# Two model blocks in one kernel on one core: plain first output tiles in RG-LRU, another order of NSA's value exchange, fourth rotation and first attention steps, and early output products

## What is computed

```python
def rglru_mixer(h, w_in, conv_w, conv_b, w_ra, b_ra, w_ix, b_ix, lam, w_out):
    u = h @ w_in                          # 1024 x 3072
    xb, yb = u[..., :D_RNN], u[..., D_RNN:]      # D_RNN = 1536
    y = jax.nn.gelu(yb)
    ...                                   # conv, two gates, a and b_t from them
    def step(hprev, inp):
        a_t, b_t = inp
        hn = a_t * hprev + b_t
        return hn, hn
    _, hs = lax.scan(step, ...)
    return (rec * y) @ w_out              # rec is hs; 1536 x 1024

def nsa_mixer(h, w_q, gate_bias, w_o, kc, vc, ks, vs, kw_pad, vw_pad):
    # 16 heads, 4 key groups; q rotated in its first 24 of 96 dims for two branches
    ...                                   # per head and block of 128 queries:
    return g_t[..., 0:1] * o_c + g_t[..., 1:2] * o_s + g_t[..., 2:3] * o_w
    ...
    return o @ w_o                        # 1024 x 1024

def moba_mixer(h, w_qkv, q_gain, k_gain, w_out):
    ...                                   # 8 heads of 128, softmax over all keys at this length
    return o @ w_out
```

## Time and profile before

| | us |
|---|---|
| runs | 1742.52, 1743.94, 1744.46 |
| the profiled execution, whole | 1750.02 |
| its span, first to last instruction | 1748.2 |
| PE busy | 1709.4 (98%), 12958 instructions |
| PEld busy | 1603.4 (92%) |
| DVE busy | 1273.3 (73%) |
| ACT busy | 838.3 (48%) |
| POOL busy | 377.2 (22%) |
| mean granted clock of PE | 0.990 |
| DMA | 321 MB, 184 GB/s in the mean |

### The profile page before, as it was taken

The page is one execution under the profiler, slowest core; times in us unless marked ns, Lnnn a source line. Parts: engine busy times, 40 slices in busy tenths (PEclk is TensorE's granted clock), DMA queues, the critical chain, the costliest instruction groups (busy, mean ns, idle before and its releaser), DMA issues.

```text
span 1748.2 us, 31974 instructions
## 1 busy us (share of the span) xinstructions
PE 1709.4 (98%) x12958; PEld 1603.4 (92%) x12958; DVE 1273.3 (73%) x1667; ACT 838.3 (48%) x1110; POOL 377.2 (22%) x425
## 2 busy tenths in 40 slices
PE   7989999999999999999999999999999999999999
PEld 7779999898779999899989989998999989989998
DVE  7898889785858988888766867666666665676663
ACT  5865444443555444454444245444444444554442
POOL 0223012535405123510032121002100127330000
PEclk9999999999899999999999999999999999999999
DMA  8236568675205778555646334554455545335561
GB/s 322 97 117 214 197 216 274 226 271 194 69 1 178 257 243 292 190 182 180 228 157 242 136 139 175 192 206 178 158 181 203 205 153 176 117 130 193 193 226 37
DMA packets 50712, 321.03 MB, mean 184 GB/s; under 512 B 7696, under 2 KB 8912, under 8 KB 20144
## 3 DMA queue, kind: packets, MB, share of 16 engines
q1 hardware_dynamic: 36432, 280.61, 45.4%
q0 software_dynamic: 12736, 36.87, 6.5%
q10 hardware_dynamic: 1440, 2.10, 0.3%
HBM read 307.39 MB, written 10.09 MB: 182 GB/s over the span
## 4 chain that ended last, share of the span: by engine, by line
PE 89%; DVE 7%; ACT 2%; issue 1%; DMA 1%; POOL 0%; ACTq 0%; DVEq 0%
PE bank L2276 18%; PE bank L2270 17%; PE bank L2271 17%; PE bank L2272 17%; PE bank L2277 9%; DVE w_lo L1445 2%; PE bank L2529 1%; PE bank L2712 1%; PE bank L2880 1%; PE bank L2832 1%; PE bank L2601 1%; PE bank L2539 1%; PE bank L2450 1%; DMA vc_other<-vc_raw 1%; ACT w_hi L1019 1%
## 5 line engine op out<-in xcount | busy, mean ns | idle before, releaser
L1445 DVE TENSOR_TENSOR w_lo<-raw,w_hi 128x1024 fp32r<-128x1024 f32 (+2 forms) x492 | 650.0, 1324 | 273.9 <-ACT w_hi L1019 272.5
L1019 ACT ACTIVATE w_hi<-raw 128x1024 fp32r<-128x1024 f32 (+2 forms) x492 | 544.1, 1113 | 605.7 <-PE bank L2272 351.0
L2270 PE MATMUL bank<-hg_hi,w_hi 128*128 128x256 f32 x2648 | 754.4, 285 | 14.1 <-DVE hg_lo L1450 10.4
L2271 PE MATMUL bank<-hg_lo,w_hi 128*128 128x256 f32 x2648 | 750.3, 283 | 0.0
L2272 PE MATMUL bank<-hg_hi,w_lo 128*128 128x256 f32 x2648 | 750.2, 283 | 0.0
L2270 PEld LDWEIGHTS bank<-hg_hi,w_hi 128*128 128x128 f32 x2648 | 509.0, 192 | 19.0 <-DVE w_lo L1445 13.7
L2271 PEld LDWEIGHTS bank<-hg_lo,w_hi 128*128 128x128 f32 x2648 | 509.2, 192 | 0.2
L2272 PEld LDWEIGHTS bank<-hg_hi,w_lo 128*128 128x128 f32 x2648 | 509.2, 192 | 0.0
L2276 PE MATMUL bank<-hid,w_hi 128*128 128x512 f32 x1056 | 372.9, 397 | 0.0
L2277 PE MATMUL bank<-hid,w_lo 128*128 128x256 f32 x1056 | 296.3, 281 | 0.0
L2276 PEld LDWEIGHTS bank<-hid,w_hi 128*128 128x128 f32 x1056 | 198.5, 188 | 48.2 <-issue 1.0
(11 more groups left out here) (407 smaller groups left out, 1930.3 us busy)
## 6 DMA issues: line engine op xcount, KB each, us to landing
raw<-in_w SPq DMA_DIRECT2D x189, 1024.0 KB, 4.9
raw<-in_w SPq DMA_DIRECT2D x48, 1408.0 KB, 6.2
raw<-in_w SPq DMA_DIRECT2D x8, 768.0 KB, 4.2
b_rows<-in_s_b_rows POOLq DMA_DIRECT2D x8, 512.0 KB, 7.7
l_rows<-s_powers POOLq DMA_DIRECT2D x64, 64.0 KB, 9.3
s_ca<-cp_s POOLq DMA_DIRECT2D x8, 512.0 KB, 5.1
s_ba<-ba_s POOLq DMA_DIRECT2D x8, 512.0 KB, 7.8
ba_slot<-s_ba POOLq DMA_DIRECT2D x8, 512.0 KB, 5.4
```

Source lines behind the costliest of these rows:

```text
L1019: act.activation(w_hi[s][:, 0:n], raw[r][:, c * n:(c + 1) * n], ACT.Copy).then_inc(hi_made, 1)
L1445: dve.tensor_tensor(w_lo[s][:, 0:n], raw[r][:, c * n:(c + 1) * n], w_hi[s][:, 0:n].bitcast(F32), ALU.subtract).then_inc(lo_made, 1)
L2270: pe.matmul(psum, w_hi_ap, x_hi_ap, start=first, stop=False, **kw)
L2271: pe.matmul(psum, w_hi_ap, x_lo_ap, start=False, stop=False, **kw)
```

## The change

- RG-LRU: tiles 0 and 1 of the output (halves 24 to 27, `PLAIN`) are no longer split. PE multiplies the raw f32 weights by the f32 `rec_f(g)`, one product per k-tile, in turns by group; DVE adds one PSUM half to h. `n_split` counts the halves that are split. SP waits for the plain products themselves before it loads units 16 and 17, and its eight loads of this size stand outside a loop. `rec_f` lies in y_gelu. The ends of ACT's and DVE's lists are in another order, with splits 28 and 29 instead of 24 to 27.
- NSA: POOL issues one compression load instead of three ahead of the exchange of kc_raw and vc_other.
- NSA: `turn_queries(6, 3)` stands behind split j = 24.
- NSA's first steps: factor(1) at the end of DVE's step 1 (`done`), behind `keep_queries(5)`; compressed maxima in step 2 behind maxima(2), compressed probabilities at step 2's end, on PE ahead of the compressed rows in step 2; ACT's compressed exps behind exps(2); DVE's last two splits in step 5.
- NSA and MoBA: output tiles 0 to 3 have banks of their own (`ATT_BANKS`), and the first products stand between the last turns and outputs (`Outward`, `behind_turns`).

The diff, cut to its core:

```diff
@@ -54,8 +54,7 @@
-GELU_AT = {19: (0, 1), 20: (2,), 21: (3,), 22: (4,)}
-FINISH_AT = (21, 22)
+ATT_BANKS = (0, 1, 2, 3, 2, 3, 2, 3)
@@ -283,6 +282,13 @@
+first = 2 * phases[0]["u0"] + 2 * RT
+PLAIN = range(first, first + SPLIT) if phases[0]["kind"] == "rglru" else range(0)
+def n_split(half):
+    return half + 1 - sum(p <= half for p in PLAIN)
@@ -339,8 +345,7 @@
-    slot = GT * (g % 2)
-    return xb[:, slot:slot + GT, 0:T]
+    return y_gelu[:, GT * g:GT * g + GT, :]
@@ -639,7 +644,10 @@
-            sp.wait_ge(lo_made, 2 * (unit - RAW) + 2 + 2 * row_step * it)
+            if 2 * (unit - RAW) in PLAIN:
+                sp.wait_ge(half_used, 2 * (unit - RAW) + 2)
+            else:
+                sp.wait_ge(lo_made, n_split(2 * (unit - RAW) + 1) + 2 * row_step * it)
@@ -672,7 +680,7 @@
-        if run >= 2 * BODY:
+        if run >= 2 * BODY and not any(2 * (unit + i) in PLAIN for i in range(run)):
@@ -849,15 +857,14 @@
-        for i in range(3):
-            load_compression(i)
+        load_compression(0)
-        for i in range(3, 6):
+        for i in range(1, 6):
@@ -1015,7 +1022,8 @@
-            act.wait_ge(half_used, half - SPLIT + 1 + 2 * BODY * it)
+            before = half - SPLIT
+            act.wait_ge(half_used, (before - SPLIT if before in PLAIN else before) + 1 + 2 * BODY * it)
@@ -1064,7 +1072,8 @@
-                split_hi(half0 + m * per_tile + j + SPLIT)
+                if m or half0 not in PLAIN:
+                    split_hi(half0 + m * per_tile + j + SPLIT)
@@ -1152,7 +1161,7 @@
-        for j in range(2 * RT):
+        for j in range(2 * RT - SPLIT):
@@ -1163,10 +1172,13 @@
-            for u in GELU_AT.get(j, ()):
-                gelu_of_y(u)
-            if j in FINISH_AT:
-                hi_of_rec(FINISH_AT.index(j))
+        for u in range(4):
+            gelu_of_y(u)
+        hi_of_rec(0)
+        gelu_of_y(4)
+        split_hi(half0 + 2 * RT + SPLIT)
+        split_hi(half0 + 2 * RT + SPLIT + 1)
+        hi_of_rec(1)
@@ -1283,7 +1295,6 @@
-            compressed_exps(0)
@@ -1292,8 +1303,8 @@
-        attention(att, {7: lambda: compressed_exps(1)},
-                  {1: last_weights, 2: lambda: compressed_probs(0), 3: last_rows, 10: lambda: compressed_probs(1)})
+        attention(att, {2: lambda: compressed_probs(0), 7: lambda: compressed_exps(1)},
+                  {1: last_weights, 2: lambda: compressed_exps(0), 3: last_rows, 10: lambda: compressed_probs(1)})
@@ -1441,7 +1452,7 @@
-        dve.wait_ge(hi_made, half + 1 + 2 * BODY * it)
+        dve.wait_ge(hi_made, n_split(half) + 2 * BODY * it)
@@ -1478,8 +1489,11 @@
-    def add_to_h(ph, m, psum):
+    def add_to_h(ph, m, psum, parts=2):
+        if parts == 1:
+            dve.scalar_tensor_tensor(h[:, m, :], psum[:, 0:T], ph["scale"], h[:, m, :], ALU.mult, ALU.add).then_inc(h_written, 1)
+            return
@@ -1489,11 +1503,13 @@
-            if per_tile == 2:
+            plain = half in PLAIN
+            if per_tile == 2 and (m or not plain):
-            add_to_h(ph, m, bank[banks[m % 2]])
-            split_lo(half + per_tile - 1 + SPLIT)
+            add_to_h(ph, m, bank[banks[m % len(banks)]], 1 if plain else 2)
+            if m or not plain:
+                split_lo(half + per_tile - 1 + SPLIT)
@@ -1731,8 +1747,6 @@
-            if g >= 2:
-                dve.wait_ge(rec_made, g - 1)
@@ -1782,21 +1796,18 @@
+        times_y(0)
+        keep_y(4)
-        dve.wait_ge(xc_made, 4)
-        times_y(0)
-        split(24)
-        lo_of_rec(0)
-        keep_y(4)
-        split(25)
-        lo_of_rec(1)
-        split(26)
+        lo_of_rec(0)
+        times_y(3)
+        split(28)
+        lo_of_rec(1)
+        split(29)
-        split(27)
-        times_y(3)
@@ -1805,7 +1816,7 @@
-    def attention(att, at_step, behind_maxima={}):
+    def attention(att, at_step, behind_maxima={}, done=()):
@@ -1847,10 +1858,12 @@
-            if n >= 1:
+            if n >= 1 and n - 1 not in done:
+            if n in done:
+                factor(n)
@@ -2008,22 +2021,17 @@
-            if j == 25:
+            if j == 24:
-        def last_queries():
-            compressed_maxima(0)
-            keep_queries(5)
-            compressed_probs(0)
-        attention(Attention("nsa"), {1: last_queries, 2: last_weights,
+        attention(Attention("nsa"), {1: lambda: keep_queries(5), 2: lambda: compressed_probs(0), 5: last_weights,
-                  {1: lambda: masked_scores(0)})
-        project(ph, half0 + 28, 1)
+                  {1: lambda: masked_scores(0), 2: lambda: compressed_maxima(0)}, (1,))
+        project(ph, half0 + 28, 1, ATT_BANKS)
@@ -2068,7 +2076,7 @@
-        project(ph, half0 + 24, 1)
+        project(ph, half0 + 24, 1, ATT_BANKS)
@@ -2278,7 +2286,7 @@
-        pe.wait_ge(lo_made, half + 1 + 2 * BODY * it)
+        pe.wait_ge(lo_made, n_split(half) + 2 * BODY * it)
@@ -2388,7 +2396,7 @@
-                pe.wait_ge(lo_made, half + 1 + 4 * it)
+                pe.wait_ge(lo_made, n_split(half) + 4 * it)
@@ -2454,22 +2462,30 @@
+            def plain(m, g, used=0):
+                for k in range(GT * g, GT * g + GT):
+                    half = half0 + 2 * m + k // 6
+                    r, at = half // 2 % RAW, half % 2 * half_size(half) + k % 6 * P
+                    pe.wait_ge(recf_made, g + 1)
+                    pe.wait_ge(raw_loaded[r], 16 * (half // (2 * RAW) + 1))
+                    last = pe.matmul(bank[REC_BANKS[m]][:, 0:T], raw[r][:, at:at + P], rec_f(g)[:, k % GT, :],
+                                     start=k == 0, stop=k == RT - 1)
+                if used:
+                    last.then_inc(half_used, used)
-                    if m == 0:
+                    if m == 2:
-            part(0, range(6), 1)
-            part(1, range(6))
-            part(0, range(6, 9))
-            part(1, range(6, 9))
-            part(0, range(9, RT), 2)
-            part(1, range(9, RT), 1)
+            for g, used in enumerate(((0, 0), (1, 0), (0, 0), (2, 1))):
+                plain(0, g, used[0])
+                plain(1, g, used[1])
@@ -2513,7 +2529,28 @@
-    def attention(att, score, pv, step_waits, after_scores, at_step):
+    class Outward:
+        def __init__(self, ph, half0, x, per_group, jobs):
+            self.ph, self.half0, self.x, self.per_group, self.jobs = ph, half0, x, per_group, jobs
+        def part(self, m, ks):
+            hi, lo = weights(self.half0 + m)
+            for k in ks:
+                if m == 0:
+                    pe.wait_ge(o_made, self.jobs + 2 * (k // self.per_group) + 2)
+                last = wide_passes(bank[ATT_BANKS[m]], hi[:, k * P:(k + 1) * P], lo[:, k * P:(k + 1) * P],
+                                   self.x[:, :, k, :], k == 0, k == KT - 1)
+            if k == KT - 1:
+                last.then_inc(half_used, 1)
+        def rest(self):
+            for m in range(2, KT):
+                if m >= 4:
+                    pe.wait_ge(h_written, h_count(self.ph["hw"], m - 2))
+                self.part(m, range(KT))
+    def attention(att, score, pv, step_waits, after_scores, at_step, behind_turns):
@@ -2564,6 +2601,8 @@
+            if n in behind_turns:
+                behind_turns[n]()
@@ -2722,6 +2761,12 @@
+        outward = Outward(ph, half0 + 28, hq, 2, job_n["nsa"])
+        def first_tiles():
+            outward.part(0, range(4, 6))
+            outward.part(1, range(2))
@@ -2730,14 +2775,18 @@
+            compressed_probs(0)
-                  {0: lambda: pe.wait_ge(sc_read, 4), 1: lambda: compressed_probs(0),
-                   2: rows_and_kept, 3: lambda: compressed_turn(1), 4: lambda: pe.wait_ge(sc_read, 8), 9: lambda: compressed_probs(1), 10: lambda: kept_compressed(1)})
-        project(ph, half0 + 28, 1, 8, hq,
-                lambda k: pe.wait_ge(o_made, job_n["nsa"] + 2 * (k // 2) + 2))
+                  {0: lambda: pe.wait_ge(sc_read, 4),
+                   2: rows_and_kept, 3: lambda: compressed_turn(1), 4: lambda: pe.wait_ge(sc_read, 8), 9: lambda: compressed_probs(1), 10: lambda: kept_compressed(1)},
+                  {14: lambda: outward.part(0, range(4)), 15: first_tiles})
+        outward.part(1, range(2, 6))
+        outward.part(0, range(6, 8))
+        outward.part(1, range(6, 8))
+        outward.rest()
@@ -2805,15 +2854,20 @@
+        outward = Outward(ph, half0 + 24, mo_o, 4, job_n["moba"])
-        attention(att, score, pv, step_waits, lambda: values(3), {0: all_keys, 1: all_values})
-        project(ph, half0 + 24, 1, 8, mo_o,
-                lambda k: pe.wait_ge(o_made, job_n["moba"] + 2 * (k // 4) + 2))
+        attention(att, score, pv, step_waits, lambda: values(3), {0: all_keys, 1: all_values},
+                  {3: lambda: outward.part(0, range(4))})
+        outward.part(1, range(4))
+        outward.part(0, range(4, 8))
+        outward.part(1, range(4, 8))
+        outward.rest()
```

## The result

The changed kernel takes 1732.13 us in the median of 4 runs (1731.03 to 1733.8), the kernel before, run beside it, 1743.23 (4 runs): ratio 0.9939, 95% interval 0.9921 to 0.9956, some 11 us less. The forecast was 22.7 less, 1721. The sign is right and 1732 lies in the range, but the size is off by a factor of two: 11.6 us have to be found.

What follows compares the result with a forecast made beforehand. PE is busy for 98% of the span, so time comes only from its idle gaps, lower-clock stretches and work removed. Terms 6.6 + 3.4 + 6.7 + 4.8 + 1.2 = 22.7 us, from 1743.9 to 1721.2; range 1715 to 1733.

Steps and rivals of the forecast that it cites:

- RG-LRU: RG-LRU's output: 24 plain f32 products at 0.44 us each remove the waits for rec and the half-clock stretch; 6.6 us gained.
- SP's later loads: Behind RG-LRU, SP's units 16 to 18 load some 4 us later: costed at nothing; as a rival 1725, chance 0.04.
- The exchange: NSA's values: with 1 MB less ahead in POOL's queue, vc_other lands earlier; 1.8 plus half of 3.4 us, 3.4 gained.
- SP's share: NSA's values: SP's loads hold the exchange only by half; rival: they keep it from landing earlier, 1725, chance 0.05.
- NSA's first steps: NSA's attention: earlier fourth rotation and new step order remove waits of 1.5 and 2.0 and 5.1 of low clock; 6.7 us.
- a clock of 0.5 in the steps: Sign for NSA's first steps: half clock seen there would make that 6.7 us step wrong.
- rivals 1 and 3: 1: the clock falls again in NSA's first steps, costing 3.4 us: 1725, chance 0.17; 3: see Rival 3.
- Rival 3: NSA's attention: POOL's later rotations hold DVE at maxima(2) to (4), 1 us each: 1724, with a lock to 1728; chance 0.06.
- Early outputs: Output products moved into waits at attention's end: 4.8 us in NSA, 3.0 of it clock, and 1.2 in MoBA.
- The base: Whole kernel: terms summed against the profiled execution (1750.02), 6.1 us above the median of 1743.94 from which the gain was taken.

## Why the prediction was half right

**RG-LRU: right.** 7.0 in the trace and 6.7 by the medians alone, against 6.6; absence of a gap and clock as worked out, the pitch 0.424 us where the forecast had 0.44. (24 at 0.44 are 10.6 us, not the 10.4 of the sum; its end at 117.8 goes by 10.6. Measured were 10.2.) In all six profiles of kernels without the part 6.8 us at half clock follow the wait for `rec`; with it there are none. SP's later loads cost nothing: PE has no wait for them.

**The exchange: the mechanism right, the term too large.** The landing fell from between 5.5 and 7.6 us to between 3.2 and 4.8, over all profiles. Half of the 3.4 us were the stretch at 0.52, and of the six profiles without this part only that of before has it. PE's waits there, L2511's and that for a late weight of the compression, are 1.8 us in before and 2.6, 1.1, 0.7, 0.3 and 0 in the others, 1.1 in the mean. With 0.3 for the clock that is 1.4 us, and 2.3 (0.2 to 4.2) were measured. That the table has 3.4 against 3.4 is luck of the one profile of before. The Trainium skill (DMA: Bandwidth & Descriptors, "Queues, rings and completion order") has each queue served in order; with POOL's two 512 KB loads behind the exchange instead of ahead of it the landing went from 7.6 to 3.5 us, which agrees. The runs changed only POOL's queue, so they say nothing on SP's share.

**NSA's first steps: the step that failed.** It reads: "The splits at step 5 (2.3 us) meet a DVE with 1.1 us to spare against PE there; I find factor(5) and (6) still in time because max(5) no longer waits." Two things in it were wrong. The splits took 4.5 us, not 2.3. And the 1.1 us to spare were gone before they began, since factor(4) ahead of them had lost 2.1 us to POOL (1.06 and 1.03). The order of the work was not wrong in itself: with POOL's last rotations cut short the splits fit at step 5. Nor is the place behind the rotations enough: at step 7, in 2.35 us, they still cost PE 2.5 us. Half clock followed the wait of 3.3 us (6.9 us at 0.51, worth 3.4), together 6.7 of the 7.1 that went missing; that a clock of 0.5 in the steps would make this step wrong, the prediction had said itself. Moving the two splits out of the way brought back 7.0.

So rivals 1 and 3 came together, and priced one by one neither reached 1732. Rival 3 was the right mechanism in the wrong place: I looked for POOL's rotations over maxima(2) to (4), 1 us each, and priced the splits, which stand in the same stretch, from rows without POOL. The rows of before could have told me. One is the small product at 1.10 and 0.16 us; I used it for a rival and not for the sum. The other I did not use at all: the same two splits, at step 2 beside POOL's rotation, took 3.44 us there and not 2.3 (DVE's timeline, before):

```profile
455.64 3.44 DVE L1445 TENSOR_TENSOR w_lo<-raw,w_hi 128x1024 fp32r<-128x1024 f32 x2
```

In the trace of after the two engines take turns: POOL's instruction ends at 456.65, the first split at 457.7, POOL's next at 458.85, the second split at 459.9, each 1.1 us behind the other, about what a split takes alone (1.2). The Trainium skill (SBUF — State Buffer, "Who interferes with whom") has a lock for whole instructions; these turns, and the 2.28 us of a split beside POOL against 1.2 without, agree with it.

**The same term was too large in its clock, too.** For the 10.3 us at 0.51 I took 5.1. In five profiles with the steps and splits in their old order, or only the splits moved, the 1.97 us wait at turn(1) is there each time. In three (before, RG-LRU alone, splits alone moved) the clock falls at once, for 10.2 us, and PE, slower, waits no more. In two (exchange alone, outputs alone) it stays up, PE catches up with DVE and waits 1.5 us again, and then only 3.4 us are low (PE's timeline, exchange alone):

```profile
457.38 1.96 PE L2538 MATMUL bank<-na_tab,prob 128*128 128x128 f32 x8 [1.50 <-DVE prob L1833]
```

That is 5.1 us in the one case and 1.5 + 1.7 = 3.2 in the other, 4.3 in the mean.

**Early outputs: right.** 5.3 and 0.9 in the trace, 5.3 by the medians alone, against 6.0. The 6.9 us at 0.52 were worth 3.0 in the profiled execution; in the other five profiles without the part the stretch is 6.8, 6.8, 3.4, 0 and 0.

**The base.** I took clock gains from one execution and their sum from a median 6 us below it. The profiled execution had 34 us at half clock; the mean clock of 23 runs of before, 0.994, means 2 x 0.006 x 1741, some 21 us, so 6.5 us of time less (their median span is 6.9 us below the profiled one). Of that, by the profiles above, some 1.4 (exchange), 0.8 (first steps) and 1 (outputs) were in my sum, and with 0.7 for the gap at L2511 that is 3.9 us. With 7.1 for step 5 it makes 11.0 of the 11.6 us between 22.7 and the measured 11.1. The first figure is shown by the moved splits; the second rests on five or six profiles a place and is an estimate.

**A version that beats both**: the changed kernel with `9: last_weights` on DVE, 1725.45 us, 18 less than before.

## What to carry to other kernels

When work is moved on DVE, its price is read from rows of the stretch that it moves into, and there first from what POOL does in that time; an instruction of POOL beside it doubled a split. Idle time of an engine is only room for a filler if the filler lands in it: at step 7 the splits stood ahead of factor(7), for which PE waits, and the idle time lay behind it. (The splits right behind factor(7), at step 8, were not run.) And a clock gain is priced from several executions: the long waits (1.97, 2.77 and 3.27 us here) come back each time to a tenth of a microsecond, short ones less well, and the half-clock stretches behind them do not.

## What was not expected of the hardware

- The same wait, of 1.97 us in each of five profiles, was followed by 10.2 us at half clock in three and by 3.4, some 6 us later and behind a second wait, in two. A wait of 1.2 to 1.3 us at scores(4), in five profiles, was followed by 6.8 us at 0.53 in that with the short rotations, and by none in the other four.
- After has 3.4 us at 0.50 behind PE's 2.77 us wait for `w_lo` at the start of an FFN (739.53, PE's timeline). All fourteen profiles have this wait, 2.77 or 2.78 us long (before at 755.10), and six have the stretch: both of the changed kernel, those with RG-LRU, the steps or the outputs alone, and the steps with splits at 9. Before and seven others keep the full clock. The two waits for `glu` at 1014.6 and 1016.6 (1.4 and 1.0 us, in every profile) are followed by 6.8 us at half clock in four, before among them, by 3.4 in eight, after among them, and by none in two. So a stretch that one of two profiles has is not yet an effect of the change; for the one at 739.7 it stays open.

```profile
739.53 0.48 PE L2278 MATMUL bank<-hg_hi,w_hi 128*128 128x256 f32 x1 [2.77 <-DVE w_lo L1456]
```

- A plain f32 product of 128x128 by 256 takes 0.424 us at full clock, only a fifth more than the pair of 512 and 256 columns that it replaces (0.355).
